# Two meeting points taken out around the MLPs of the first block, and the mean of the following layer norm accumulated inside the last MLP group

## The reference, cut to what matters

```python
for i in range(2):
    m = hybrid_mixer(...) if i == 0 else mla_mixer(...)
    h = layer_norm(ALPHA * x + m, ln1_g[i], ln1_b[i])
    f = square(relu(h @ mlp_w1[i])) @ mlp_w2[i]              # 1024 -> 4096 -> 1024
    e = sigmoid(h @ ple_w_gate[i]) * (p[i] @ ple_w_proj[i])  # the "gate stage"; p[i] is 512 x 256
    x = layer_norm(ALPHA * h + f + e, ln2_g[i], ln2_b[i])    # mean, then variance, over 1024
```

## Time and profile before

| | |
|---|---|
| median of 3 runs | 3409.42 us (3407.19 to 3414.97) |
| the profiled execution, its own time | 3412.91 us |
| its span | 3410.7 us |
| TensorE matmul busy | 3214.5 us (94%) |
| VectorE busy | 1580.3 us (46%) |
| ScalarE busy | 1218.6 us (36%) |
| GpSimd busy | 79.0 us (2%) |
| mean granted TensorE clock | 0.961 of 2.4 GHz |

### The profile page before, as it was taken

One profiled execution on the slowest core, in us unless ns is written; L12 is line 12 of the kernel. 1 busy time (PEld: TensorE's weight loads), 2 busy tenths in 40 slices (PEclk: granted clock), 3 DMA queues, 4 the chain that ended last, 5 costly groups with the idle time before them and its releaser, 6 DMA issues. The chain is left out here.

```text
span 3410.7 us, 39289 instructions
## 1 busy us (share of the span) xinstructions
PE 3214.5 (94%) x15200; PEld 2509.8 (74%) x15200; DVE 1580.3 (46%) x2389; ACT 1218.6 (36%) x2022; POOL 79.0 (2%) x84
## 2 busy tenths in 40 slices
PE   7898999999899999998998998999999987999999
PEld 5676677774377677775886786788888874778887
DVE  3653466662144466665523643433333434344444
ACT  2243333332354333334413453422222334543332
POOL 3100000000000000000000200000000000000000
PEclk9858999999999999999999998999999999999999
DMA  4201344341210144431121000112111110022221
GB/s 162 75 1 50 120 151 160 125 170 28 50 62 26 52 183 158 162 150 47 57 62 50 1 1 25 50 50 74 55 68 65 58 50 25 1 74 92 86 93 74
DMA packets 160796, 259.43 MB, mean 76 GB/s; under 512 B 58476, under 2 KB 73194, under 8 KB 160556
## 3 DMA queue, kind: packets, MB, share of 16 engines
q1 hardware_dynamic: 158932, 252.94, 21.1%
q10 hardware_dynamic: 1628, 4.76, 0.4%
q0 software_dynamic: 128, 0.26, 0.0%
HBM read 255.85 MB, written 2.10 MB: 76 GB/s over the span
## 5 line engine op out<-in xcount | busy, mean ns | idle before, releaser
L1190 ACT ACTIVATE w_hi<-wbuf 128x1024 fp32r<-128x1024 f32 x330 | 348.4, 1058 | 1232.4 <-PE psA L750 1184.0
L748 PE MATMUL psA<-act_hi,w_hi 128*128 128x512 f32 (+1 forms) x1824 | 694.8, 381 | 60.1 <-DVE act_lo L1801 32.9
L749 PE MATMUL psA<-act_lo,w_hi 128*128 128x512 f32 (+1 forms) x1824 | 683.1, 375 | 0.0
L750 PE MATMUL psA<-act_hi,w_lo 128*128 128x512 f32 (+1 forms) x1824 | 681.7, 374 | 0.0
L1795 DVE TENSOR_TENSOR w_lo<-wbuf,w_hi 128x1024 fp32r<-128x1024 f32 x330 | 404.0, 1227 | 551.6 <-ACT w_hi L1190 547.2
L748 PE MATMUL psA<-hid_hi,w_hi 128*128 128x512 f32 (+1 forms) x1280 | 476.6, 372 | 3.3 <-DVE work L1902 0.2
L749 PE MATMUL psA<-hid_lo,w_hi 128*128 128x512 f32 (+1 forms) x1280 | 472.0, 369 | 0.0
L750 PE MATMUL psA<-hid_hi,w_lo 128*128 128x512 f32 (+1 forms) x1280 | 471.2, 368 | 0.0
L748 PEld LDWEIGHTS psA<-act_hi,w_hi 128*128 128x128 f32 x1824 | 349.4, 192 | 132.7 <-issue 52.2
L749 PEld LDWEIGHTS psA<-act_lo,w_hi 128*128 128x128 f32 x1824 | 349.4, 192 | 62.1 <-issue 3.6
L750 PEld LDWEIGHTS psA<-act_hi,w_lo 128*128 128x128 f32 x1824 | 348.8, 191 | 61.2
(11 more groups left out here) (230 smaller groups left out, 3580.4 us busy)
## 6 DMA issues: line engine op xcount, KB each, us to landing
wbuf<-in_mlp_w_dram SPq DMA_DIRECT2D x64, 2048.0 KB, 8.2
work<-in_ada_w_dram SPq DMA_DIRECT2D x32, 1536.0 KB, 10.9
wbuf<-in_ab_w_in_dram SPq DMA_DIRECT2D x10, 1024.0 KB, 5.0
wbuf<-in_ple_w_gate_dram SPq DMA_DIRECT2D x4, 2048.0 KB, 7.7
wbuf<-in_hy_w_in_dram SPq DMA_DIRECT2D x3, 2048.0 KB, 8.0
wbuf<-in_c_w_in_dram SPq DMA_DIRECT2D x3, 2048.0 KB, 7.6
wbuf<-in_hy_w_out_dram SPq DMA_DIRECT2D x2, 2048.0 KB, 7.5
wbuf<-in_mla_w_out_dram SPq DMA_DIRECT2D x2, 2048.0 KB, 7.7
```

What stands on the lines that cost most here:

```text
L748: pe.matmul(psA[:, s, a:b], w_hi, x_hi[:, a:b], start=first, stop=False)
L749: pe.matmul(psA[:, s, a:b], w_hi, x_lo[:, a:b], start=False, stop=False)
L750: ins = pe.matmul(psA[:, s, a:b], w_lo, x_hi[:, a:b], start=False, stop=last)
L1190: return nc.scalar.activation(out, in_, func, **kw)
```

## The change

Five edits, for `mlp0` and `mlp1` alike:

1. The two meetings at each MLP are gone (four in all; GpSimd's own count of meetings goes from 8 to 4).
2. In their place at the front, VectorE signals `ple_set` when the gate stage's last `acc` is written, and ScalarE waits for it after `w_hi` of units 0 and 1.
3. VectorE's `w_lo` of unit 0 moves from behind the gate stage to ahead of its output 5. `w_lo` of unit 1 stays behind it.
4. The mean of `acc` is no product stage of its own any more (`ln_m1`, `ln_m3`). The last group of each MLP is written out after a loop of seven, and in it TensorE adds the mean's products, one for each of the 8 tiles, into a bank of its own (`psB[:, 1]`) as VectorE finishes the tiles (`acc_set`): five of them ahead of the group's last output, three behind it.
5. Ahead of the second layer's norm, ScalarE's 8 squares of the context half (128x256) are done 2 ahead of and 6 behind the squares that the variance waits for, instead of all 8 ahead.

```diff
@@ plan of the psA halves
-          ("ln_m1", 1), ("ln_v1", 1),
+          ("ln_v1", 1),
...
-          ("mlp1", GROUPS * (GH + KD)), ("ln_m3", 1), ("ln_v3", 1),
+          ("mlp1", GROUPS * (GH + KD)), ("ln_v3", 1),
@@ TensorE
             def layer_norm(i, x):
-                if i % 2:
-                    product(f"ln_m{i}", 0, [(0, LAT, [(C["mean"], x[:, k, 0:LAT]) for k in range(KD)])])
                 sum_squares(f"ln_v{i}", ln_squares[i], LAT)
...
                         split_products(name, [j0], n, operands, more, [range(GH)])
+                        if last:
+                            acc_mean(index, j0 - GH - 2)
...
                         if turned_at:
                             mod_turn()
+                        if last:
+                            acc_mean(index, j0 - GH - 1)
+                            if q == GH - 1:
+                                acc_mean(index, KD - 2)
+
+                if name in ADA:
+                    with pe.Fori(0, GROUPS - 1) as i:
+                        group(i, False)
+                    group(GROUPS - 1, False, True)
+                    acc_mean(index, KD - 1)
...
+            def acc_mean(l, k):
+
+                pe.wait_ge(S["acc_set"], KD * l + k + 1)
+                ins = pe.matmul(psB[:, 1, :], C["mean"], acc[:, k, :], start=(k == 0), stop=(k == KD - 1))
+                if k == KD - 1:
+                    ins.then_inc(S["acc_mean"], 1)
...
             ple(0)
-            meet(pe)
             mlp("mlp0", 0, LAT)
-            meet(pe)
             layer_norm(1, acc)
@@ ScalarE
+                if name in ADA:
+                    act.wait_ge(S["ple_set"], ADA[name] + 1)
                 with act.Fori(0, GROUPS - 1) as i:
...
-            meet(act)
-            for k in range(KD):
-                f(squares[TOK][:, k, LAT:TOK], xT[:, k, LAT:TOK], ACT.Square)
-            layer_norm(3, acc, "ln2_b", 8, xT, behind=lambda k: f(
+
+            def context_squares(ks):
+
+                act.wait_ge(S["acc_mean"], 2)
+                for k in ks:
+                    f(squares[TOK][:, k, LAT:TOK], xT[:, k, LAT:TOK], ACT.Square)
+
+            context_squares(range(2))
+            layer_norm(3, acc, "ln2_b", 8, xT, between=lambda: context_squares(range(2, KD)), behind=lambda k: f(
@@ VectorE
                 if i % 2:
-                    ps, free = get_a(v, f"ln_m{i}", 0)
+                    v.wait_ge(S["acc_mean"], i // 2 + 1)
+                    ps, free = psB[:, 1, :], S["mean_read"]
...
                 for j in range(KD):
+                    if j == 5:
+                        w_lo(f"mlp{l}", 0)
                     emptied(v, f"ple_g{l}", j)
                     ps, free = get_a(v, f"ple_p{l}", j)
                     tt(gates[:, j, :], gates[:, j, :], ps[:, 0:LAT], ALU.mult).then_inc(free, 1)
                     v.drain()
                     stt(acc[:, j, :], acc[:, j, :], ALPHA, gates[:, j, :], ALU.mult, ALU.add)
-                w_lo(f"mlp{l}", 0)
+                v.drain().then_inc(S["ple_set"], 1)
                 w_lo(f"mlp{l}", 1)
...
                         tt(acc[:, j, :], acc[:, j, :], ps[:, 0:n], ALU.add).then_inc(free, 1)
+                        if last and name in ADA:
+                            v.drain().then_inc(S["acc_set"], 1)
@@ GpSimd
-PRE_LSTM, BEFORE_MLP3 = 8, 2
+PRE_LSTM, BEFORE_MLP3 = 4, 2
```

More of the change, by code:

```diff
@@ L264, in build @@
         S = {n: sem(n) for n in (
-            "centered", "squared", "sum_ready", "sum_read", "mean_read", "norm_set", "acc_zero", "relu_used", "act_hi", "act_split", "w_hi", "w_split", "g_hi", "hidden_set",
+            "centered", "squared", "sum_ready", "sum_read", "mean_read", "acc_set", "acc_mean", "ple_set", "norm_set", "acc_zero", "relu_used", "act_hi", "act_split", "w_hi", "w_split", "g_hi", "hidden_set",
             "ada_used", "ada_sum", "row_ready", "row_set", "row_turned", "conv_set", "vec_set", "sqrt_set", "lam_exp", "lam_set",
@@ L938, in mlp, with group @@
             def mlp(name, index, n):
-                def group(i, paired):
+                def group(i, paired, last=False):
                     more = i * ((GH + KD) // 2)
@@ L972, in group @@
                             mod_turn()
-                paired = name not in ADA
-                if paired:
-                    group(0, True)
-                with pe.Fori(1 if paired else 0, GROUPS) as i:
-                    group(i, False)
+                        if last:
[7 more added lines that the diff above has]
+                    acc_mean(index, KD - 1)
+                else:
+                    group(0, True)
+                    with pe.Fori(1, GROUPS) as i:
+                        group(i, False)
+            def acc_mean(l, k):
[3 more added lines that the diff above has]
+                    ins.then_inc(S["acc_mean"], 1)
             def mod_rows(l, i):
@@ L1288, in inverse_root, with layer_norm @@
                 f(dst, dst, ACT.Exp, scale=-0.5).then_inc(free, 1)
-            def layer_norm(i, x, bias, j0, dst, x_hi=None, ahead=(), behind=None):
+            def layer_norm(i, x, bias, j0, dst, x_hi=None, ahead=(), behind=None, between=None):
                 for a in ahead:
@@ L1295, in layer_norm @@
                     f(squares[LAT][:, k, :], x[:, k, 0:LAT], ACT.Square).then_inc(S["squared"], 1)
+                if between:
+                    between()
                 inverse_root(f"ln_v{i}", 0, rstd[:, 0:LAT], LAT, eps_ln)
@@ L2100, in _ @@
             ple(0)
-            meet(v)
             mlp("mlp0", 0, LAT)
-            meet(v)
             layer_norm(1, acc, "ln2_g", 0, xT)
```

## The result

The changed kernel took 3425.02 us (median of 6 runs, 3421.13 to 3428.2), the kernel before, run beside it, 3410.69 (6 runs, 3407.19 to 3414.97). The ratio is 1.0041, with a 95% interval of 1.0028 to 1.0054: slower, by 14 us or 0.4%. Forecast were 3422.7 us (3414 to 3430) and +13.3.

What follows compares the result with a forecast made beforehand. TensorE, busy 94% of the span, was taken to bound the kernel. Front ends +15.0 us (6.3 + 5.3 + 2 x 1.7) and back ends -1.7 gave +13.3 on the median 3409.4: 3422.7 us, range 3414 to 3430.

Steps and rivals of the forecast that it cites:

- Output 7: End of the projection: TensorE idles 6.6 us, starts output 7 at 403.75, ends it 8.1 us later (`mlp1` 7.9).
- Units 0 and 1: First MLP units: start right behind the projection, take 10.9 to 11.0 us, through at 418.1, then some 5.5 waiting.
- Queue: Second chunk and modulation weights, queued behind output 7, issued 8.1 us later; the latter take 11.3, landing at 418.9.
- Unit 2: Third MLP unit waits for its `w_lo`, ready at 423.6 in `mlp0`; starts 6.3 us later, 5.3 in `mlp1`.
- The second idle stretch: TensorE ahead of unit 2: idle 4.5 to 5.5 us, clock falls, costing 1.7 per MLP, bounds 0 and 2.7.
- The back end: Mean behind each MLP: the meeting's 0.83 us idle goes, twice, -1.7 in all; bounds 0 and -1.8 each.
- Edit 5: ScalarE's context squares ahead of the second layer's norm: covered, cost nothing; if the cover went, up to 1.9 once.
- it spreads: Rival, chance 0.07: a later `w_lo` in the first group is late again, TensorE stops once more per MLP; 3430.
- queue not late: Rival, chance 0.08: VectorE's stall delays the projection, but modulation weights land in time for unit 2; 3408, 1 us faster.
- no stall: Rival, chance 0.05: first MLP weights are there when VectorE comes, TensorE goes on without a gap; gain 6.2, 3403.

Runs made afterwards that it cites:

- the modulation weights first: Changed kernel with group 0's two modulation-weight transfers issued ahead of the second weight chunk, split still ahead of output 5: 3410.86 us, ratio 0.9992 to the kernel before.
- split behind: Changed kernel with edit 3 undone, so `w_lo` of unit 0 stands behind the gate stage again: 3405.69 us, ratio 0.9981 to the kernel before.
- back end alone: Kernel before with edit 1 behind the MLPs only, plus edits 4 and 5; meetings ahead of the MLPs kept: 3406.53 us, ratio 0.9989.
- both queue and split: Changed kernel with edit 3 undone and group 0's modulation weights issued ahead of the second chunk: 3409.43 us, ratio 0.9990 to the kernel before.
- one chunk: Changed kernel with the projection's weights in one chunk and modulation weights ahead of the second MLP chunk: 3397.14 us, ratio 0.9959 to the kernel before.
- edit 3 alone: Kernel before with only `w_lo` of unit 0 moved ahead of output 5, meetings and mean as before: 3426.24 us, ratio 1.0035.
- one chunk and the split behind: Changed kernel with one projection chunk, modulation weights ahead of the second MLP chunk, edit 3 undone: 3410.04 us, ratio 0.9983 to the kernel before.

## Why the prediction was right, step by step

All in us into the stretch, `mlp0` / `mlp1`.

- *Output 7.* Forecast to start 18.59 / 18.37 in (403.75 - 385.16; 1200.25 - 1181.88); it started at 17.91 / 18.27, because ScalarE had its weights 0.6 sooner in `mlp0`. The idle time ahead of it was 5.7 / 6.1; the forecast's own rows give 6.4 (403.75 less 397.3, where seven of the eight outputs end), not the 6.6 it states. It ended 7.8 later than before, forecast 8.1 / 7.9. The 3.45 at half clock was 3.78 / 3.46. The experiment with the split before output 6 shows that it was the half of `psA`.
- *Units 0 and 1.* Unit 0 was forecast behind output 7, 22.0 / 21.8 in, and started at 20.70 / 21.07, since its row overlaps that of output 7 (which ends 21.7 in); the two units took 12.34 / 11.44 instead of 10.9 to 11.0. The two errors offset each other: TensorE was through at 33.0 / 32.5, forecast 32.9 / 32.8. Neither decides, because unit 2 waits for its `w_lo`.
- *Queue.* Both transfers 7.8 later; the first modulation product 7.7 / 7.9 later (25.59 to 33.31, 25.66 to 33.60), so the way from issue to use was 11.2 and 11.4, where I took 11.3 from before's row. By the Trainium skill, "DMA: Bandwidth & Descriptors", section "Anatomy of one DMA", which is for GpSimd's path, the estimate was 10.4: the trace of this SyncE queue gives 0.8 to 1.0 more. The 32 landings had a minimum of 10.6 and a median of 10.9.
- *Unit 2.* Forecast +6.3 and +5.3, measured +5.98 (32.13 to 38.11) and +5.35 (32.95 to 38.30). With the modulation weights first it was +0.7 and -0.2, the forecast's +0.8 and -0.2 for that case. This step is shown.
- *The second idle stretch* was 4.9 and 5.6, forecast 4.5 to 5.5, and the clock fell in both. Its price is read from unit 2 to the subtraction: 379.31 / 379.09 here, and 376.87 / 377.33 on average over the four traces with the new back end and no such stretch (split behind, back end alone, both queue and split, one chunk). That is 2.4 and 1.8 where I took 1.7 each: 0.8 too little, within the bound of 2.7. The timeline agrees: the first 12 matmuls of unit 2 took 5.24 us in `mlp0` and the first 8 took 3.54 in `mlp1`, 2.5 and 1.7 more than at 0.23 each. No run filled this second idle time, so its price is read and was not taken away by an edit. The Trainium skill's advice against idle gaps ("TensorE: Matmul & The Clock Gate", "Why this matters for your kernels") agrees with these two stretches; the 3.8 us and one place with 3.24 us kept full clock.
- *The back end.* The same two means against before's 377.50 / 377.50: -0.6 and -0.2, where I took -0.83 each: 0.9 too much, within the bound of 0. In `mlp1` the changed kernel waits longer than before at eight places (waits of TensorE, 1190 to 1610 us: waiting engine, tile and line, releaser, total, times, longest):

```profile
PE psA L699 <- DVE work L1904: 6.1, 1, 6.1
PE psA L748 <- DVE w_lo L1812: 5.6, 1, 5.6
PE psA L748 <- DVE work L1922: 1.5, 8, 0.2
PE psA L912 <- ACT work L1201: 1.5, 1, 1.5
```

  The third row, eight waits of 0.19 for VectorE's additions, is also there with the back end alone and absent with edit 3 alone, so it belongs to edits 1, 4 and 5. Before, TensorE stood at the same eight places too, for 0.10 us. The first of them, before and then after:

```profile
1230.93 0.39 PE L750 MATMUL psA<-hid_hi,w_lo 128*128 128x512 f32 x1
1231.42 0.50 PE L748 MATMUL psA<-hid_hi,w_hi 128*128 128x512 f32 x1
...
1239.45 0.39 PE L750 MATMUL psA<-hid_hi,w_lo 128*128 128x512 f32 x1
1240.03 0.47 PE L748 MATMUL psA<-hid_hi,w_hi 128*128 128x512 f32 x1 [0.19 <-DVE work L1922]
```

  From start to start 0.49 became 0.58: 0.09 more, eight times, 0.7 us. That takes up nearly all of the 0.83 in `mlp1`, where 0.2 was won. In `mlp0` one such wait of 0.19 stands, and 0.6 was won. The idle gap of the meeting went as forecast; a term for these waits was missing. That they come from one stage less in the plan of the `psA` halves, which swaps the halves for what follows, is argued and was not tried apart.
- *Edit 5* was costed at nothing. Timeline of ScalarE behind `mlp1`, against the earlier trace rows:

```profile
1600.70 0.72 ACT L1201 ACTIVATE work<-xT 128x256 f32<-128x256 f32 x2 [5.40 <-PE psB L991]
...
1606.14 1.93 ACT L1201 ACTIVATE work<-xT 128x256 f32<-128x256 f32 x6
1609.34 0.69 ACT L1201 ACTIVATE work<-psA,const 128x512 f32<-128x512 f32 x1 [1.27 <-PE psA L912]
```

  Behind its six squares ScalarE still waits 1.27 of the 3.10: they are covered, with that much to spare. From VectorE's first subtraction to this last row it took 8.64 us before (1592.33 to 1600.97) and 8.64 after (1600.70 to 1609.34): edit 5 cost nothing, as forecast.

The sum: 6.0 + 5.35 at unit 2, 2.4 + 1.8 of clock, -0.6 - 0.2 behind: +14.7, forecast +13.3. The two mis-sized terms are the clock of the second stretch (0.8) and the back end (0.9), both to the same side; unit 2 was 0.3 too high. Of the rivals, "it spreads" has nothing for it (378.23 busy of 379.13 in `mlp0`; in `mlp1` the idle time behind the start of unit 2 is the eight short waits, 1.5 us), "queue not late" fell with unit 2 at +6.0 and +5.35, and "no stall" with the 5.7 and 6.1 us. So the path, both waits and the order of the steps were right, and each term of the sum came within 0.3 us in each MLP except the clock in `mlp0` and the back end in `mlp1`, both 0.7 off.

## What to carry to other kernels

Before an operation is moved ahead of others on an in-order engine, ask when its last input arrives, and then what the operations now behind it set free: here a buffer half, by that an output, by that a transfer queue's next entry, and by that the weights for the unit after next. The same move cost 18.8 us with late weights and saved 8.2 with early ones, so first make the input early, and only then move its reader. In a queue, put the transfer whose wait is already over ahead of the one that still waits: where all was on time it changed 0.9 us, and where a stall was it took away 15.0 of 18.8 us.

## What the runs showed of the hardware that was not expected

- For stretches between 3.2 and 4 us the length did not tell whether the clock falls. 3.24 us in `mlp0` kept it and 3.23 in `mlp1` lost it, in both executions of that variant, and the fall came only as work had begun again (granted 1.00 in 1189.6 to 1192.8, 0.60 in the next 3.4 us). 3.8 us kept it, and it was 1.00 in the 3.3 us behind as well; 3.98, with the split behind in the first experiment, lost it. A fall cost 1.6 (11.0 to 12.6 for units 0 and 1) to 2.7 us.
- Code outside the stretches differs between executions by more than most edits here: the start-up by 8 us over the profiles here (377.1 to 385.2), the end by 6 (1818.4 to 1824.7 from the last subtraction on). The two stretches, read from the trace, told differences of a few us that medians of 5 to 12 runs left unclear: the one kernel that was profiled twice gave 812.0 and 812.1 for them, at total times of 3406.8 and 3403.8. Each other kernel has one trace, so differences below 1 us rest on that one pair. In the variant with one chunk and the split behind the runs fell into two groups some 9 us apart, which the one place read in two executions did not explain.
